# A fused encoder step on one core: the order of attention heads and filler work in the mixing stage is regrouped

## The reference

```python
pr = project(x, lp)                       # RMSNorm(x) @ w_in: cq, ckv, kr, mq, mk, mv, gates, mo
q = mla_queries(pr['cq'], pos, lp)        # 8 heads of 96: up-projection, rotation, RMSNorm
k, v = mla_keys_values(ckv_all, kr_all, lp)
s = jnp.einsum('bqhe,bkhe->bhqk', q, k) * MLA_SCALE
p = jax.nn.softmax(jnp.where(visible, s, -jnp.inf), axis=-1)   # block-causal, chunks of 64
att = jnp.einsum('bhqk,bkhe->bqhe', p, v)
hm, state = mlstm_run(state, mq, mk, mv, ig, logf)              # 4 heads, chunkwise recurrence
x = x + concat([att, rms_norm(hm) * sigmoid(mo)]) @ w_out
x = x + moe(rms_norm(x), lp)              # top-1 group of 4, top-2 of its 8 experts, SwiGLU
```

## Time and profile before

| | |
|---|---|
| median of the runs | 1542.9 us |
| the profiled execution | 1541.49 us |
| its span | 1539.6 us |
| TensorE matmuls busy | 1370.3 us (89%) |
| VectorE busy | 531.2 us (35%) |
| ScalarE busy | 291.1 us (19%) |
| mean granted TensorE clock | 0.94 |

### The profile page before, as it was taken

How to read it: one execution, slowest core, us unless ns; L and a number is a source line. 1 busy time by engine, 2 the same in 40 slices (tenths; PEclk the granted TensorE clock), 3 DMA queues, 4 the chain that set the end, 5 groups by cost and what they waited for, 6 DMA issues and landing times.

```text
span 1539.6 us, 37430 instructions
## 1 busy us (share of the span) xinstructions
PE 1370.3 (89%) x16424; PEld 1040.9 (68%) x16424; DVE 531.2 (35%) x1021; ACT 291.1 (19%) x623; POOL 203.8 (13%) x293
## 2 busy tenths in 40 slices
PE   5899999738888998988989737999999999999996
PEld 2444444325556556656566437999999999999995
DVE  2110100165577658647474661111111111111110
ACT  5200100043323333333332100000100000000000
POOL 3100000011122102202020001111111111111101
PEclk9999999868988999989999958999999999999998
DMA  7021110232011201101011057999999999999992
GB/s 281 14 80 40 62 57 26 78 148 71 22 57 62 70 22 49 70 22 49 17 49 42 14 235 256 350 374 378 368 369 373 375 376 365 367 364 371 369 369 59
DMA packets 40462, 274.02 MB, mean 178 GB/s; under 512 B 9848, under 2 KB 13816, under 8 KB 28108
## 3 DMA queue, kind: packets, MB, share of 16 engines
q1 hardware_dynamic: 33232, 255.33, 43.3%
q0 software_dynamic: 7168, 17.84, 4.8%
HBM read 248.40 MB, written 32.05 MB: 182 GB/s over the span
## 4 chain that ended last, share of the span: by engine, by line
PE 71%; DVE 13%; DMA 6%; issue 5%; ACT 3%; POOL 1%; SPq 0%; DVEq 0%; POOLq 0%; ACTq 0%
PE psum L981 20%; PE psum L737 15%; PE psum L1007 10%; PE psum L830 8%; DMA arena<-in_w 5%; PE psum L868 3%; PE psum L880 2%; PE psum L691 2%; PE psum L900 2%; PE psum L1017 2%; DVE small L1756 2%; PE psum L972 1%; PE psum L777 1%; DVE arena L1772 1%; DVE arena L542 1%
## 5 line engine op out<-in xcount | busy, mean ns | idle before, releaser
L981 PE MATMUL psum<-arena 128*64 128x96 f32 x8192 | 359.6, 247 | 7.6 <-issue 3.8
L981 PEld LDWEIGHTS psum<-arena 128*64 128x64 f32 x8192 | 347.5, 137 | 17.7 <-issue 14.1
L737 PE MATMUL psum<-arena 128*128 128x512 f32 (+1 forms) x576 | 238.5, 575 | 0.0
L737 PEld LDWEIGHTS psum<-arena 128*128 128x128 f32 x576 | 109.1, 191 | 123.7 <-issue 123.7
L1007 PE MATMUL psum<-arena 128*64 128x96 f32 x4096 | 176.9, 245 | 1.1 <-issue 1.1
L1007 PEld LDWEIGHTS psum<-arena 128*64 128x64 f32 x4096 | 173.1, 136 | 1.5 <-issue 1.5
L830 PE MATMUL psum<-arena 128*128 128x512 f32 x288 | 128.8, 601 | 1.9 <-DVE arena L1780 1.3
L691 PE MATMUL psum<-ident,arena 128*128 128x128 f32 (+1 forms) x432 | 70.7, 312 | 64.2 <-DVE arena L1613 33.7
L691 PEld LDWEIGHTS psum<-ident,arena 128*128 128x128 f32 (+1 forms) x432 | 57.0, 152 | 88.1 <-DVE arena L1613 40.1
L1303 ACT ACTIVATE arena<-psum,slot_gate 96x1024 f32<-96x1024 f32 x32 | 35.6, 1111 | 386.7 <-PE psum L1017 386.7
L830 PEld LDWEIGHTS psum<-arena 128*128 128x128 f32 x288 | 55.6, 194 | 68.5 <-issue 64.8
(11 more groups left out here) (225 smaller groups left out, 1336.4 us busy)
## 6 DMA issues: line engine op xcount, KB each, us to landing
arena<-in_w SPq DMA_DIRECT2D x96, 2048.0 KB, 19.0
arena<-in_x_rows SPq DMA_DIRECT2D x18, 512.0 KB, 5.3
z_rows<-arena SPq DMA_DIRECT2D x9, 980.0 KB, 4.6
arena<-in_w_in SPq DMA_DIRECT2D x1, 7840.0 KB, 23.5
arena<-z_rows SPq DMA_DIRECT2D x9, 768.0 KB, 5.3
out_y<-arena SPq DMA_DIRECT2D x9, 512.0 KB, 2.6
xn_rows<-arena SPq DMA_DIRECT2D x9, 512.0 KB, 2.9
arena<-in_w_out SPq DMA_DIRECT2D x1, 4096.0 KB, 17.2
```

Source lines behind the costliest of these rows:

```text
L737: ins = pe.matmul(o[:, 0:hi - lo], xT[s][:, k, :], w_in[:, k, lo:hi], start=(k == 0), stop=(k == KD - 1))
L981: ins = pe.matmul(o[c:c + CT, j * EB:(j + 1) * EB], w[:, k, j * P + c:j * P + c + CT], x[:, k, :], start=(k == 0), stop=(k == KD - 1))
```

## The change

Four things change. Within a step, TensorE issues the scores of the next unit before the transposes of this one, and VectorE takes the next maximum before it copies this unit's transposed probabilities. Across tiles, the scores, maximum and exponentials of the next tile's first unit are issued at the end of the tile, on TensorE ahead of the last values. `filler` moves the pieces: cqT runs one tile earlier (tile n + 2, at step 7), q0 and q1 go from step 3 to 0, ckvT from 2 to 0, qbT and kbT from 2 to 1, kn and v with the sums from 4 to 2, qkm from 3 to 2, kq from 6 to 3, o1 from 2 to 3, xnorm from 3 to 4, the transposes of queries and keys from 7 and 8 to 4 and 6, and lg from 6 to 7. For n = -1 a list of its own stands, the old one with cqT of tile 1 added at step 8. `attention_out` goes behind the pieces of step 0. And `sums_inverse` inverts eight columns (four in tile 0) and then spreads them by a copy.

```diff
+    if n < 0:
+        return {
+            0: [], 1: [("cqT", 0)], 2: [("ckvT", m)], 3: [("q0", 0), ("q1", 0)],
+            4: [("kn", m), ("v", m), ("qsum", 0), ("ksum", m)], 5: [], 6: [("kq", m)], 7: [("qTa", 0), ("qTb", 0)],
+            8: [("kTa", m), ("kTb", m), ("cqT", 1)],
+        }[h]
     return {
-        0: [("mxb", n - 1)] * old + [("gt", n), ("nm", n)] * now,
-        1: [("o0", n - 1)] * old + [("cqT", n + 1)] * nxt,
-        2: [("o1", n - 1)] * old + [("qbT", n), ("kbT", n)] * now + [("ckvT", m)] * nxt,
-        3: [("q0", n + 1), ("q1", n + 1)] * nxt + [("qkm", n), ("ua", n), ("ub", n)] * now + [("xnorm", n - 1)] * old,
-        4: [("kn", m), ("v", m)] * nxt + [("ia", n), ("na", n)] * now + [("qsum", n + 1)] * nxt + [("ksum", m)] * nxt,
+        0: [("mxb", n - 1)] * old + [("q0", n + 1), ("q1", n + 1)] * nxt + [("gt", n), ("nm", n)] * now
+           + [("ckvT", m)] * nxt,
+        1: [("o0", n - 1)] * old + [("qbT", n), ("kbT", n)] * now,
+        2: [("kn", m), ("v", m)] * nxt + [("qkm", n)] * now + [("qsum", n + 1), ("ksum", m)] * nxt,
+        3: [("kq", m)] * nxt + [("o1", n - 1)] * old + [("ua", n), ("ub", n)] * now,
+        4: [("qTa", n + 1), ("qTb", n + 1)] * nxt + [("ia", n), ("na", n)] * now + [("xnorm", n - 1)] * old,
         5: [("ib", n), ("nb", n)] * now + [("xna", n - 1), ("xnb", n - 1)] * old + [("hsq", n)] * now,
-        6: [("kq", m)] * nxt + [("lg", n - 1)] * old,
-        7: [("qTa", n + 1), ("qTb", n + 1)] * nxt + [("hout", n)] * now,
-        8: [("kTa", m), ("kTb", m)] * nxt,
+        6: [("kTa", m), ("kTb", m)] * nxt,
+        7: [("lg", n - 1)] * old + [("hout", n)] * now + [("cqT", n + 2)] * (n + 2 < NT),
+        8: [],
     }[h]
...
@@ TensorE (ScalarE's exps are moved across the tile in the same way)
-                if now:
+                if n == 0:
                     scores(n, 0)
...
                             values(n, h // 2 - 1)
-                        probs_transposes(n, unit_at(n, h))
                         if unit_at(n, h) + 1 < units(n):
                             scores(n, unit_at(n, h) + 1)
+                        probs_transposes(n, unit_at(n, h))
                 for key in filler(n, HA):
                     step(key)
+                if now and n + 1 < NT:
+                    scores(n + 1, 0)
                 if now:
                     values(n, HA // 2 - 1)
...
@@ VectorE
-                dve.reciprocal(rinv.rearrange("p (u c) -> p u c", u=k),
-                               bc(rsum[:, 0:k], [P, k, BANK // k])).then_inc(rinv_ok, 1)
+                link(dve.reciprocal(rsum_inv[:, 0:k], rsum[:, 0:k]))
+                dve.tensor_copy(rinv.rearrange("p (u c) -> p u c", u=k),
+                                bc(rsum_inv[:, 0:k], [P, k, BANK // k])).then_inc(rinv_ok, 1)
...
-                if n >= 1:
-                    attention_out(n - 1)
...
                     for key in filler(n, h):
                         fill_work(key)
+                    if n >= 1 and h == 0:
+                        attention_out(n - 1)
                     if now and unit_at(n, h) is not None:
-                        pT_take(n, unit_at(n, h))
                         if unit_at(n, h) + 1 < units(n):
                             row_max(n, unit_at(n, h) + 1)
+                        pT_take(n, unit_at(n, h))
                 if now:
                     sums_inverse(n)
                 for key in filler(n, HA):
                     fill_work(key)
+                if now and n + 1 < NT:
+                    row_max(n + 1, 0)
```

More of the change, by code:

```diff
@@ L375, in build @@
         rsum = tiny(HA)
+        rsum_inv = tiny(HA)
         ropet = tiny(2 * ROPE)
@@ L1286, in _ @@
                     fill_work(key)
+                if now and n + 1 < NT:
+                    exps(n + 1, 0)
             act.wait_ge(r_dve, 1)
```

## The result

The changed kernel is slower: a median of 1553.1 us (1550.8 to 1557.0) beside 1541.9 (1539.7 to 1544.9) of the kernel before on the same chip, a ratio of 1.0074 (95% interval 1.0052 to 1.0095). Its profiled execution took 1553.1 us, with a span of 1551.2. The prediction said 1524, with 1503 to 1546.

A forecast was written before the change was run, and what follows sets the result against it. The prediction took the mixing stage to be paced by TensorE. A full-clock gain of 32 us less 13 us for the clock left 19, taking 1541.5 to 1522.5 us, 1524 on the median's level, range 1503 to 1546.

The forecast's parts named there:

- The walk: Tile 5 followed piece by piece on TensorE and VectorE at full clock: period 57.0 us against 62.0, 5.0 less.
- The full-clock walk: Walks of tiles 5 and 2 without 1.2 GHz stretches: mean gain 3.5 us, 25 over tiles 1 to 7.
- Tile 2's walk: The same walk with tile 2's shorter pieces: period 48.9 us against 51.0, 2.1 less, with VectorE setting the pace.
- two thirds of 33 us: Share of the mixing stage's work added at 1.2 GHz taken as staying; with 0.6 on the path, 13 us.
- a gain of 5: Tile 0: about 5 us saved, after a start 1.1 us later.
- The first wait of the earlier trace: Tile 0's TensorE wait of 4.78 us for cqT's keys, which was to go.
- the second: Tile 0's TensorE wait of 5.62 us for kq, which was to stay for the most part.
- The signs: Profile checks: tile 5 near 57 to 59 us, tile 2 near 50, clock 0.94 to 0.96; wrong if under 0.91.
- The three waits of tile 5: TensorE idle before ia 1.1 us, before step 6 values 2.1, before the last values 1.75.
- More time at 1.2 GHz: Rival: clock falls at two gaps per tile, 80 us added, 48 on path, 1559 us; decides from 4.0 a tile; 12 in 100.
- VectorE's later copies eat it: Rival: light-stretch values and ring transposes wait 1 us more, 24 us in all: 1541 to 1546, no change; 10 in 100.
- Clock stays up: Rival: no half-clock stretch left in the light stretch of a tile, so the full 32 us: 1511 us; 17 in 100.

The follow-up runs named there:

- e7: Changed kernel with hsq, the norm of the mLSTM output, moved from step 5 to 6: 1532.3 us, 0.9925 of the kernel before.
- e2b: Changed kernel plus two throwaway 128x512 products per tile in the gap at step 6: 1541.7 us, 1.0004 of the kernel before.
- e3: Changed kernel with cqT moved from step 7 to the end of step 6: 1543.2 us, 1.0000 of the kernel before.
- e5: Kernel before with only the eight-column reciprocal and its spreading copy: 1535.5 us, 0.9949 of the kernel before.
- e6: Kernel before with only the new order of scores, transposes, maximum and copy within a step: 1533.5 us, 0.9944 of the kernel before.
- e1: Changed kernel with VectorE copying transposed probabilities before taking the next maximum: 1545.9 us, 1.0017 of the kernel before.
- e10: Changed kernel with the old piece lists, keeping the border and the later attention_out: 1546.6 us, 1.0023 of the kernel before.
- e11: Kernel before with the new reciprocal and the new order within a step, old lists, no border: 1528.4 us, 0.9896 of the kernel before.
- e17: Changed kernel with hsq at step 6 and attention_out in its old place, border kept: 1523.9 us, 0.9896 of the kernel before.
- e16: Changed kernel without the border, attention_out in its old place, hsq at step 6: 1537.3 us, 0.9981 of the kernel before.

## Why the prediction was wrong

The forecast was 1522.5 us on the level of the profiled execution, which took 1553.1: 30.6 us missed. The parts:

**Where tile 5 was missed.** The walk had 57.0 us, the trace 62.55. Of the 5.5 us, 4.3 lie in one stretch, from the values of step 6 to the last values: 9.4 us in the walk (25.7 - 16.3), 13.7 in the trace. At full clock, in e7 and e2b, that stretch takes 10.9 us. So 1.5 us are the walk's error and 2.8 the clock's. Another 0.7 us lie before it: from the end of the second half to the values of step 6 the walk had 16.3 us, the trace 17.0.

**The full-clock walk, 15 us.** At about half of 43 us on the path, the stage after would last 477.3 - 21 = 456 us at full clock; the walks made it 468.3 - 25 - 2 = 441. The step that failed is the cost of cqT at step 7, "on VectorE a copy and six small operations, 1.9 us", behind "GpSimd's power (0.9)". Here are e7's rows of cqT's first and last operation on VectorE, and then GpSimd's power and what GpSimd did beside the last:

```profile
665.97 0.42 DVE L1632 TENSOR_TENSOR arena<-psum,small 128x256 f32<-128x256 f32 x1
...
668.58 0.65 DVE L1624 TENSOR_TENSOR arena<-arena,small 128x32 f32<-128x32 f32 x1
```

```profile
665.03 0.34 POOL L1348 TENSOR_SCALAR small<-small 128x2 f32<-128x2 f32 x1 [2.81 <-ACT arena L1170]
665.46 1.14 POOL L1350 TENSOR_TENSOR small<-small 128x2 f32<-128x2 f32 x1
...
668.57 0.61 POOL L1404 COPY arena<-arena 128x512 f32<-128x512 f32 x1
```

cqT takes 3.3 us on VectorE, and the power 1.6; less the 0.6 us in which the two overlap, they are 4.2 us beside the 2.8 of the walk, which is the 1.5 us but for 0.1. In the kernel after itself cqT took as long (3.3 us) in tiles 0 and 6, but 2.0 to 2.3 in tiles 1 to 5: there VectorE reached it late, behind lg at 1.2 GHz, with the power long done. So in those tiles the clock took what cqT would have taken, and the split between this part and the next is one of full clock against the rest, not of two causes that add. That cqT at step 7 costs is shown by e3 all the same, which wins 0.7% back by moving it. Tile 2's walk missed more: 48.9 us, where e7 has 52.1 at a clock of 0.97 and hsq's 1.3 us are to be added back. There the last wait is 3.53 us in e2b instead of the 2.6 walked; which other items make up the rest wasn't taken apart. The mean of the two walks carried the error to all seven tiles.

**The clock, 8 us.** The forecast kept two thirds of 33 us and put 0.6 of them on the path, 13 us. 43 us were lost instead of 22, and about half of them cost time (0.46 in e2b, about half in e7). The share on the path was nearly right; that the loss would shrink was wrong. The walk had placed the wait before the values of step 6 at 2.1 us, 2.26 in the trace, and then priced the clock by a share of the old loss instead of by what stands right behind that wait.

**Tile 0, 7 us.** Forecast was a gain of 5; the first output projection starts 2.1 us later than in the earlier trace rows. The first wait of the earlier trace rows went and the second became 3.77 us, as said. But cqT of tile 2, 3.3 us of VectorE, now stands ahead of the row sums of tile 0:

```profile
392.85 1.11 PE L916 MATMUL psum<-ident,arena 128*128 128x128 f32 x4 [4.05 <-DVE arena L1784]
...
401.47 0.70 PE L837 MATMUL psum<-arena 128*128 128x512 f32 x1 [1.69 <-DVE arena L1792]
```

The price of cqT in the open was walked for the other tiles and not for this one, and the wait for `attention_out` was dismissed with "the work of step 0 and the second head's scores lie before it". They do, but by the rows of tile 5 the nm step before it on VectorE waits for ScalarE's gate rows, and the first half waits 1.69 us in tile 0, 1.31 in tile 2 (where the walk had 2.1) and 0.34 in tile 5 (where it had none).

15 + 8 + 7 is the 30 us. The first two are estimates from e7 and e2b, since no run holds the clock at 2.4 GHz throughout.

**The signs.** Tile 5's period (57 to 59 us forecast) was 62.6, tile 2's (near 50) 57.1, the clock of the stage (0.94 to 0.96) 0.91. The two signs by which the forecast was to be seen as wrong hardly showed: a clock under 0.91, and a last gap of more than 3 us, which stands in tile 6 alone (3.05 us), a tile that gained.

**What was right.** The reciprocal with its copy:

```profile
L1784 DVE COPY arena<-small 128x512 f32<-128x512 f32 x9 | 3.8, 428 | 0.3
...
L1783 DVE RECIPROCAL small<-small 128x8 f32<-128x8 f32 x8 | 1.5, 186 | 0.0
```

0.66 us together with the wait between them (forecast 0.7), worth 0.5% by itself (e5). Scores ahead of transposes is worth 0.6% by itself (e6). kq ends at 656.5, before the second half, and nobody waits for it in tiles 1 to 7. The three waits of tile 5 came where they were walked: 0.98 us before ia (forecast 1.1), 2.26 (2.1), 1.26 (1.75, 3.4 at full clock).

**The rivals.** "More time at 1.2 GHz" had the mechanism: e2b shows that the falls behind the step-6 gap cost time and that work laid in the gap brings it back. But its size was 80 us lost and 48 on the path; measured are 43 and about 20, 2.5 us a tile and under the 4.0 from which it was to decide. It decides only together with the missing full-clock gain. "VectorE's later copies eat it" is partly right: the copies ahead of the maximum (e1) win 0.6% back against the kernel after, though with new waits for exponentials. "Clock stays up" fell: the clock dropped to 0.50 right behind waits of 2 to 3 us for VectorE copies, with no DMA among the releasers. The Trainium skill's page "TensorE: Matmul & The Clock Gate", section "Loop structure matters more than you think", has the clock lost in long waits for DMA and kept through a VectorE copy behind which the next matmuls follow at once. Here no DMA was waited for, so the fall does not need one. The page's case of the copy is not this one: TensorE stood 2.26 us until the copy was done.

**The lists and the border.** These interact, which the forecast didn't consider. The border costs 1.3% with the old lists (e10 against e11, `attention_out`'s place included). With the new lists it pays: e17 is 0.9% under e16, which differs by the border alone.

## What to carry to other kernels

A gap on the engine that sets the pace costs its own length and, on TensorE, the slower work right behind it: price the clock by what stands behind each predicted gap, not as a share of the old loss, and as a risk, since gaps of like length left the clock up in tiles 6 and 8. Walk the busiest helper engine item by item, with the durations of operations when their neighbours run too, and walk the first tile as well. Before regrouping a whole loop, time the parts: here two small edits together gave 1.0%, the new lists alone took 0.7% away, and one piece moved by a step gave 1.5% back.

## What the runs showed of the hardware

- The granted clock went to 1.2 GHz behind waits of 2.26 us (tile 5) and 2.98 us (tile 2) for a VectorE copy, and in tile 5 it stayed there for ten microseconds although TensorE was fully busy in them. Behind waits of 1.28 us (e1), 0.80 us (e7) and 0.54 us (e2b) at the same place in tile 5 it stayed at 2.4 GHz.
- The length of the wait alone does not tell. In the kernel after, waits of 2.07 us (tile 6) and 2.74 us (tile 8) at that place left the clock at 1.00. In tile 6 it fell to 0.50 behind the 3.05 us before the last values, and in e2b it stayed at 1.00 behind 3.06 us there.
- Throwaway matmuls of 1.9 us in such a gap made the kernel after 0.7% faster. The same matmuls at a place without the gap made the kernel before 1.2% slower.
- A copy that spreads 8 values over 512 columns takes 0.43 us from SBUF, beside 0.68 for 512 columns read from PSUM (L549).
- VectorE's operation of 32 columns at L1624 took 0.65 us where GpSimd's copy at L1404 started beside it (tiles 2, 4, 5 and 6 of e7), and 0.19 where that copy was over (tiles 1 to 5 of the kernel after).
